# A two-layer hybrid decoder trunk on eight cores: 1/rms applied when PSUM is emptied, mixers reordered, one output projection, FFN results in a ring

## The reference

```
h    = rmsnorm(x) * g1                 # x * rsqrt(mean(x^2)+eps), over the 2048 channels
proj = h @ w_in                        # 2048 -> 4352 = 512 | 768 768 768 | 768 768
y_pool  = per group of 128: (window mean - token) @ pool_w * scale        # windows 2,4,8,16
y_sconv = B * causal_conv3(C * H)                                         # three 768 slices
y_cconv = silu(rmsnorm(causal_conv31(a * sigmoid(b)) + bias) * gc)        # norm over 768
x   += concat(y_pool, y_sconv, y_cconv) @ w_out
h2   = rmsnorm(x) * g2
up   = causal_conv3(h2 @ w_up)         # 2048 -> 2 x 5632
x   += (silu(up_left) * up_right) @ w_down
```

## Time and profile before

| | |
|---|---|
| time, median of 3 runs | 3723.16 us (3722.08 to 3724.32) |
| span of the profiled execution, slowest core | 3729.4 us |
| spans of the eight cores | 3711.1 to 3729.4 us |
| busy: PE, DVE, ACT, POOL | 3322.6, 2094.5, 531.7, 571.4 us |
| chain that ended last: PE, DVE, issue, DMA, ACT | 82%, 11%, 3%, 2%, 1% |
| w_up transfers: size, time to landing | 512 KB, 8.0 us |

### The profile page before, as it was taken

How to read it: one execution, slowest core, us unless ns; L and a number is a source line. 1 busy time by engine, 2 the same in 40 slices (tenths; PEclk the granted TensorE clock), 3 DMA queues, 4 the chain that set the end, 5 groups by cost and what they waited for, 6 DMA issues and landing times.

```text
span 3729.4 us, 51409 instructions; the slowest of 8 cores (3711.1 to 3729.4 us)
## 1 busy us (share of the span) xinstructions
PE 3322.6 (89%) x18974; PEld 1736.0 (47%) x19348; DVE 2094.5 (56%) x3179; ACT 531.7 (14%) x694; POOL 571.4 (15%) x602
## 2 busy tenths in 40 slices
PE   4799985799999999999859999768999999999994
PEld 3355442345555555445425554334555555544542
DVE  4533466566565565566564345657656555556556
ACT  2100002122011121112010000121212012011102
POOL 0111100111111211221201110010121121121120
PEclk7799998899999999999979999988999999999997
DMA  6276621467767767757717663144776766776752
GB/s 139 28 75 66 65 31 14 46 57 66 68 64 71 67 61 69 65 56 68 82 20 72 60 69 42 14 45 43 71 67 63 71 62 64 71 67 57 70 63 105
DMA packets 823905, 228.97 MB, mean 61 GB/s; under 512 B 809428, under 2 KB 821068, under 8 KB 821196
## 3 DMA queue, kind: packets, MB, share of 16 engines
q0 software_dynamic: 756064, 191.14, 55.7%
q1 hardware_dynamic: 63312, 32.75, 3.6%
q10 hardware_dynamic: 4284, 1.77, 0.2%
HBM read 402.17 MB, written 17.15 MB: 112 GB/s over the span
## 4 chain that ended last, share of the span: by engine, by line
PE 82%; DVE 11%; issue 3%; DMA 2%; ACT 1%; DVEq 0%; ACTq 0%; SPq 0%
PE pA L332 38%; PE pB L332 37%; DVE sb_hT L386 2%; PE pB L629 2%; PE pA L629 2%; DVE sb_sq L365 2%; DVE sb_rstd L380 1%; DVE sb_arena L496 1%; DVE sb_arena L642 1%; DVE sb_xT L787 1%; DMA sb_arena<-xp 1%; PE pA L374 1%; DVE sb_xT L807 1%; PE pB L374 0%; DMA o_ffn_s<-sb_arena 0%
## 5 line engine op out<-in xcount | busy, mean ns | idle before, releaser
L332 PE MATMUL pA<-sb_hT,sb_wr 128*128 128x512 bf16 (+1 forms) x5740 | 1017.0, 334 | 66.0 <-DVE sb_hT L386 35.1
L332 PE MATMUL pB<-sb_hT,sb_wr 128*128 128x512 bf16 (+1 forms) x5739 | 1014.0, 333 | 60.1 <-DVE sb_hT L386 32.3
L332 PEld LDWEIGHTS pA<-sb_hT,sb_wr 128*128 128x128 bf16 x5856 | 520.7, 99 | 542.7 <-issue 96.2
L332 PEld LDWEIGHTS pB<-sb_hT,sb_wr 128*128 128x128 bf16 x5856 | 519.3, 99 | 535.5 <-issue 87.5
L496 DVE SCALAR_TENSOR_TENSOR sb_arena<-sb_arena,sb_vecs 128x1056 f32<-128x1056 f32 x752 | 627.9, 835 | 80.3 <-DVE sb_arena L496 1.4
L332 PE MATMUL pB<-sb_arena,sb_wr 128*128 128x512 bf16 (+1 forms) x2819 | 521.7, 336 | 48.8 <-DVE sb_xT L787 28.3
L332 PE MATMUL pA<-sb_arena,sb_wr 128*128 128x512 bf16 (+1 forms) x2829 | 522.7, 337 | 46.8 <-DVE sb_xT L787 27.9
L332 PEld LDWEIGHTS pB<-sb_arena,sb_wr 128*128 128x128 bf16 x2880 | 259.2, 100 | 285.0 <-issue 68.0
L332 PEld LDWEIGHTS pA<-sb_arena,sb_wr 128*128 128x128 bf16 x2880 | 259.1, 100 | 285.0 <-issue 68.8
L320 POOL DMA_DIRECT2D sb_wr<-w_up x176 | 201.3, 1144 | 1155.2 <-PE pA L332 566.8
L320 POOL DMA_DIRECT2D sb_wr<-w_down x256 | 214.2, 839 | 738.5 <-PE pB L332 369.9
(11 more groups left out here) (96 smaller groups left out, 1468.8 us busy)
## 6 DMA issues: line engine op xcount, KB each, us to landing
sb_wr<-w_up POOLq DMA_DIRECT2D x176, 512.0 KB, 8.0
sb_wr<-w_in POOLq DMA_DIRECT2D x68, 512.0 KB, 7.2
sb_wr<-w_down POOLq DMA_DIRECT2D x128, 192.0 KB, 4.1
sb_wr<-w_down POOLq DMA_DIRECT2D x128, 160.0 KB, 3.8
sb_wr<-w_out POOLq DMA_DIRECT2D x64, 192.0 KB, 4.3
sb_arena<-xp SPq DMA_DIRECT2D x8, 1024.0 KB, 9.8
yp<-sb_arena SPq DMA_DIRECT2D x8, 1024.0 KB, 6.1
sb_wr<-w_out POOLq DMA_DIRECT2D x32, 128.0 KB, 3.5
```

What stands on the lines that cost most here:

```text
L332: S.op("pe", lambda e, k=k, c0=c0, n=n: e.matmul(ps[:, c0:c0 + n], lhsT=lhs_fn(k), rhs=rhs_fn(k)[:, c0:c0 + n], start=(k == 0), stop=(k == ...
```

## The change

**1/rms at eviction.** `hT` is written as x * g alone, on ACT (`h_part`), behind each addition to `xT`. The 1/rms, `R0`, is multiplied in on DVE when a PSUM tile is emptied (`mul_r`), or into the second factor of a product. ACT's copies out of PSUM go (FFN, pooling, C, and the sigmoid is taken from SBUF), and the first tap of the FFN convolution goes from DVE to ACT.

**Squares.** `SumSq.add` squares a block on ACT and adds it to a running sum on DVE, behind each chunk of the output projection and of the last down group; `finish` adds over channels with three matmuls, then square root and reciprocal. `mid_stats` puts `finish` behind the eighth block of the first chunk of the next stage. For the first layer the squares, the ones matmuls and the square root are taken per input tile, of which four instead of three are in flight.

**Order.** Conformer convolution first, then short convolution 0 to 2 with the conformer's norm in it, pooling 3 to 0, short convolution 3 to 5, then one output projection 16 blocks deep. The work buffers E are 1218 columns wide instead of 1704, and mixer and FFN results share a ring of 16 slots.

**FFN.** Down groups of 11, 11, 11, 5 and 6 pieces, each behind the up chunks that it needs, with no up group between. State loads and stores go by four pieces, the stores right behind the fourth.

The core of the diff (lines in their order, cut):

```
-GF = 6
+FG = [(0, 11), (11, 11), (22, 11), (33, 5), (38, 6)]
+NF = 44
...
+        deferred.clear()
+        for j, k in enumerate(order):
             for (c0, n) in BLKS:
...
+                S.op("pe", lambda e, j=j, k=k, c0=c0, n=n: e.matmul(
+                    ps[:, c0:c0 + n], lhsT=wr[:, base + k, :], rhs=rhs_fn(k)[:, c0:c0 + n],
+                    start=(j == 0), stop=(j == nk - 1)),
+                    reads=wres + rhs_res(k), writes=[psn])
+            if mid is not None and j == mid[0]:
+                mid[1]()
+        for f in pend:
+            f()
+        return psn
...
+    class SumSq:
+        def __init__(self, n, acc, sqs, fin, fin_res):
+            self.n, self.acc, self.sqs = n, acc, sqs
+            self.fin, self.fin_res = fin, fin_res
+            self.i = 0
+        def add(self, src, src_res):
+            i = self.i
+            self.i += 1
+            if i == 0:
+                act(self.acc.ap[:, 0:T], src, AF.Square, src_res, self.acc.res)
+                return
+            q = self.sqs[i % len(self.sqs)]
+            act(q.ap[:, 0:T], src, AF.Square, src_res, q.res)
+            last = i == self.n - 1
+            dve_tt(self.fin if last else self.acc.ap[:, 0:T], self.acc.ap[:, 0:T], q.ap[:, 0:T], ALU.add,
+                   self.acc.res + q.res, self.fin_res if last else self.acc.res)
+        def finish(self, out, out_res, inv_n):
+            psn = next_ps()
+            ps = PS[psn]
+            for (c0, n) in BLKS:
+                S.op("pe", lambda e, c0=c0, n=n: e.matmul(ps[:, c0:c0 + n], lhsT=onesB[:], rhs=self.fin[:, c0:c0 + n],
+                                                          start=True, stop=True),
+                     reads=self.fin_res + ["onesB"], writes=[psn])
+            act(out, ps[:, 0:T], AF.Sqrt, [psn, "epsT"], out_res, bias=epsT[:], scale=inv_n)
+            S.op("dve", lambda e: e.reciprocal(out=out, in_=out), reads=out_res, writes=out_res)
...
+    def norm_sum():
+        return SumSq(16, tb[1], [E[0], E[1]], E[2].ap.bitcast(BF16)[:, 0:T], E[2].res)
+    def h_part(gname, c):
+        act(hT[:, c, :], xT[:, c, :], AF.Copy, [("x", c), "vecs"], [("h", c)], scale=V(gname, c))
+    def add_x(psn, dc):
+        ps = PS[psn]
+        dve_tt(xT[:, dc, :], ps[:, 0:T], xT[:, dc, :], ALU.add, [psn, ("x", dc)], [("x", dc)])
...
+            xv = xT[:, half * 8:(half + 1) * 8, col0:col0 + n]
+            xres = [("x", c) for c in ks]
+            gv = V(("n1g", 0), half * 8, 8).unsqueeze(2).to_broadcast([128, 8, n])
+            dve_tt(hT[:, half * 8:(half + 1) * 8, col0:col0 + n], xv, gv, ALU.mult, xres + ["vecs"], [("h", c) for c in ks])
+            act(SQB[:, half * 8:(half + 1) * 8, 0:n], xv, AF.Square, xres, [("sqb", half)])
...
+            for kc in ks:
+                S.op("pe", lambda e, ck=ck, kc=kc, n=n: e.matmul(
+                    pC[:, ck * 512:ck * 512 + n], lhsT=onesB[:], rhs=SQB[:, kc, 0:n], start=(kc == 0), stop=(kc == 15)),
...
+        act(R0[:, col0:col0 + n], pC[:, ck * 512:ck * 512 + n], AF.Sqrt, [cres, "epsT"], ["R0"], bias=epsT[:], scale=1.0 / D)
+    S.op("dve", lambda e: e.reciprocal(out=R0[:], in_=R0[:]), reads=["R0"], writes=["R0"])
+    for b in E:
+        zero(b.ap, b.res + [("sqb", 0), ("sqb", 1)])
...
+        for (d0, dn, e0, sh) in ((0, NP, 0, 1), (NP, NS, s_off, 16)):
+            for i in range(3):
...
+                d = dst[:, d0:d0 + dn]
+                if i == 0 and first == "act":
+                    act(d, src, AF.Copy, ext_res + ["vecs"], dst_res, scale=w)
+                elif i == 0:
+                    dve_ts(d, src, w, ext_res + ["vecs"], dst_res)
...
+                    dve_stt(d, src, w, d, ext_res + ["vecs"] + dst_res, dst_res)
+    def mul_r(out, ps_ap, lo, hi, psn, res):
+        dve_tt(out, ps_ap, R0[:, lo:hi], ALU.mult, [psn, "R0"], res)
...
+            psn = proj(w_in_d, l, o4 + D_CC + i * 128, mid=mid_stats() if i == 0 else None)
...
+            act(Eb.ap[:, VS:VS + 480], pc, AF.Copy, cres, Eb.res)
+            mul_r(sg.ap, ps[:, 0:T], 0, T, psn, sg.res)
+            act(sg.ap, sg.ap, AF.Sigmoid, sg.res, sg.res)
+            for f in pending:
                 f()
...
+            dve_tt(sg.ap, sg.ap, R0[:], ALU.mult, sg.res + ["R0"], sg.res)
...
+        def sconv(i, after_c=(), after_h=(), l=l):
...
+            psn = proj(w_in_d, l, o1 + D_SC + i * 128)
...
+            mul_r(g.ap, ps[:, 0:T], 0, T, psn, g.res)
+            dve_tt(g.ap, g.ap, R0[:], ALU.mult, g.res + ["R0"], g.res)
+            for f in after_c:
...
+            psn = proj(w_in_d, l, o1 + 2 * D_SC + i * 128)
...
+            dve_tt(g.ap, g.ap, R0[:], ALU.mult, g.res + ["R0"], g.res)
+            for f in after_h:
+                f()
+            psn = proj(w_in_d, l, o1 + i * 128)
...
+        sconv(0, after_c=pending[:])
+        pending.clear()
+        deferred.append(lambda: csum.finish(tb[1].ap, tb[1].res, 1.0 / D_CC))
+        sconv(1, after_c=[lambda: cc_norm_out(0)], after_h=[lambda: cc_norm_out(1)])
+        sconv(2, after_c=[lambda: cc_norm_out(2), lambda: cc_norm_out(3)], after_h=[lambda: cc_norm_out(4), lambda: cc_norm_out(5)])
+        for b in PE_:
+            zero(b.ap[:, 0:16], b.res)
+        for g in (3, 2, 1, 0):
+            pool_group(g)
...
+        for i in range(3, 6):
+            sconv(i)
...
+        order = [10 + i for i in range(6)] + [0, 1, 2, 3] + [4 + i for i in range(6)]
...
+        for dc in range(16):
+            psn = chunk(wcols(w_out_d, l, 0, 16, dc * 128), 16, order,
+                        lambda k: slot(kslot[k]), lambda k: slres(kslot[k]))
+            add_x(psn, dc)
+            nsum.add(xT[:, dc, :], [("x", dc)])
+            h_part(("n2g", l), dc)
...
+                if ectr["i"] <= 3:
+                    zero(Eb.ap[:, 0:2], Eb.res)
+                psn = proj(w_up_d, l, side * D_FF + f * 128, mid=mid_stats() if first else None)
+                ps = PS[psn]
+                mul_r(Eb.ap[:, 2:2 + NP], ps[:, 0:NP], 0, NP, psn, Eb.res)
+                mul_r(Eb.ap[:, FS_OFF + 32:FS_OFF + 160], ps[:, NP:T], NP, T, psn, Eb.res)
+                S.op("dve", lambda e, Eb=Eb, ch=ch: e.transpose(out=oT3[:, ch, :], in_=Eb.ap[:, FS_OFF + 128:FS_OFF + 160]),
+                     reads=Eb.res, writes=oTX.res)
...
+                conv3(tb[side].ap, Eb.ap, FS_OFF, "fw", l, uc, Eb.res, tb[side].res, "act")
+                if side == 0:
+                    act(tb[0].ap, tb[0].ap, AF.Silu, tb[0].res, tb[0].res)
+            m = f % 16
+            dve_tt(slot(m), tb[0].ap, tb[1].ap, ALU.mult, tb[0].res + tb[1].res, slres(m))
+            if fi == 3:
...
+        def ffn_down(g, nxt, l=l):
+            f0, nf = FG[g]
+            last = g == len(FG) - 1
+            ns = norm_sum() if last else None
...
+                psn = chunk(w_down_d[l, f0 * 128:(f0 + nf) * 128, dc * 128:(dc + 1) * 128].rearrange("(kc p) c -> p kc c", p=128),
+                            nf, range(nf), lambda k: slot((f0 + k) % 16), lambda k: slres((f0 + k) % 16))
+                add_x(psn, dc)
+                if last:
+                    ns.add(xT[:, dc, :], [("x", dc)])
+                    if nxt is not None:
+                        h_part(nxt, dc)
+            if last:
+                pre_stats.append(ns)
...
+        nxt = ("n1g", l + 1) if l + 1 < DEPTH else None
+        done = 0
+        for (lo, hi, downs) in ((0, 12, [0]), (12, 23, [1]), (23, 34, [2]), (34, 44, [3, 4])):
+            for f in range(lo, hi):
+                ffn_up(f)
+            for g in downs:
+                ffn_down(g, nxt)
...
+    flush_deferred()
+    pre_stats.pop().finish(R0[:], ["R0"], 1.0 / D)
...
```

657 lines of the change are left out of this document (253 added, 404 removed).

## The result

| | before | after |
|---|---|---|
| median of the runs | 3723.74 us | 3583.48 us |
| undisturbed runs | 3722.08, 3723.16, 3724.32 | 3568.73, 3577.34, 3589.61 |
| ratio, 95% interval | | 0.960 (0.955 to 0.965) |
| profiled execution: span | 3729.4 us | 3575.8 us |

The change makes the kernel 4.0% faster: 145 us by the means of the undisturbed runs (3723.2 and 3578.6), 154 by the two profiled executions; forecast were 218.

The account below looks back on a forecast made before the run. PE was taken as the bound, busy 3322.6 of 3729.4 us, losing time to idling and a slow clock. Gains of 308 less costs of 90 made 218: 3511, less 6, 3505 us; range 3445 to 3590.

Parts of the forecast that it names:

- conformer stage: Conformer convolution: sigmoid wait goes, DVE turn about 34.5 us against PE's 30; gain 10 us (-10 to 25), both layers.
- pooling: Pooling stage: sums covered by later chunks, eviction behind the previous group's sums on DVE; 15 us lost, gain 30.
- squares: Last down group: DVE's addition, wait for square and sum take 4.27 us, chunks 5.0 with slow clock; cost 64 us.
- norms (three): Second norm (twice) and first norm of layer 1: first chunk starts at once, 10.9 us lost each; gain 109.
- start: First layer's input load ends at 72 us, second chunk starts at 87 instead of 112.5; gain 25 us (17 to 37).
- conformer norm: Norm behind the conformer: 12 us wait for the next chunk but one, 1.7 slow, 0.8 more; gain 51 us.
- FFN groups, eviction, stores: FFN: group-start losses shrink, gain 67; DVE eviction hidden at 7.85 against 8.01 us, 0; four-piece stores cost 26 (0 to 100).
- end: Final norm and output: 31.7 us becomes 15.7; gain 16 us.
- The forecast's 80: FFN loss before the change: 56.2 us of waits at down groups' third chunks plus 14 slow starts of 1.7 us.
- rival B: FFN: DVE becomes the bound, mildly, at 8.9 us per up chunk; 158 us more, 3663 us; chance 0.12.
- Rival C: Last down group runs at 1.2 GHz throughout; 32 us more, 3537 us; chance 0.13.
- E: Rival: FFN stores land in time and the last down group's clock holds; 26 and 24 less, 3455 us; chance 0.12.

Follow-up runs that it names:

- The two runs on this stage: Kernel after with ACT's emptying of the prompt taps behind the first decode tap, 3532.9 us; the same with decode taps between the matrices, 3496.6 us.
- E0: Not a run: the pooling stage's buffer, into which ACT copies the state and DVE writes the eviction's product.
- reordered conformer stage: Kernel after with each conformer decode tap directly behind its diagonal matrix and ACT's emptying of the prompt taps behind them: 3496.6 us.

## Why the prediction came out 78 us too low

The direction held, and the time lies inside the range, 7 us from its slow end; of 218 us 145 came. The conformer stage lost where a gain was forecast, pooling and the FFN gave less than forecast, and that the time still lies inside the range is partly luck: the squares were priced 36 us too dear, and had they cost the 64 of the forecast, the time would have been near 3619, beyond the range. Of the forecast's own signs of being wrong two came, up chunks more than 8.01 us apart away from the stores and longer waits in the conformer stage; the load (71.3 us) and the waits for o_ffn_s (8, 14.2 us in all) stayed within theirs. The profiled executions, both read in the same way, give this for two layers:

| term | forecast | measured | how |
|---|---|---|---|
| norms (three) | +109 | +102 | lost 12.3, 12.3 and 14.5 instead of 10.9 each |
| start | +25 | +30 | second chunk at 82.3, not 87 |
| conformer norm | +51 | +38 | lost 21 instead of 14.5 |
| conformer stage | +10 | -32 | lost 47 per layer where it was 31; turns of 39.2, not 34.5 |
| pooling | +30 | +7 | lost 27.5 where it was 31; stage of 61.5, not 48.5 |
| FFN groups, eviction, stores | +67, 0, -26 | +17 | loss of 72 where it was 88.5 |
| squares, last down group | -64 | -28 | 4.13 us for twelve chunks per layer, 3.0 for four; not 5.0 for all |
| end | +16 | +15 | 19.6 us to the first scaled block, the output 3 shorter |
| sum | +218 | +149 | the spans differ by 154; 5 are in no term |

The FFN's loss is the time from the third up chunk to the end of the last down group (689.2 to 1782.1 and 2412.9 to 3503.1), less 86 chunks of 8.01 and 704 blocks of 0.50 us, less the squares: 37.2 and 34.7, 72 in all. The squares' part is what the last group's sixteen chunks take beyond 3.0 us each: 1720.1 to 1782.1 less 48.1, 14 us per layer. Before, the FFN's stretch was 755.7 to 1851.3 and 2547.9 to 3640.2 us less 87 chunks and the same blocks: 45.9 and 42.6, so 88.5. The forecast's 80 had only the waits for `xT`'s additions and their slow chunks. The conformer's is 82.3 to 318.8 us less 13 chunks and six times 14.3 us of taps, 46.5 (48.0 in layer 1, with 12 chunks); with the same 14.3, the 213.0 us of the earlier trace rows lost 31, not the 34 that the forecast had with 13.9.

**Norms and conformer norm: right. Start: nearly the time, by another way.** The waits of 8.28 and 11.65 us answer to the 8.1 and 12 that the steps gave. Only the slow chunk behind them was dearer, 2.7 to 2.8 us instead of the 1.7 of the earlier trace rows, where PE had waited 3.56 us. The conformer norm also has a wait of 3.88 us ahead of its first transposes (330.82) and a slow chunk, where the steps had 0.8. At the start PE waited for no eviction, where the forecast had the second chunk behind reciprocal and eviction: the sums stand in pC there, so pB was free at once, and pA was emptied before the third chunk's turn at 90.28; what was lost was the slow first chunk of 10.73 us.

**Conformer stage: the step that failed.** "About 34.5 us against PE's 30" was 39.2 (five turns, 114.85 to 310.75). It added DVE's instructions, but left out a wait that the change makes: the first decode tap now stands behind ACT's emptying of the prompt taps (2.83 us, 34.1 in all), since both write one slot. It also took PE's share as fixed, though PE, once it waits, runs its transposes and taps slowly: 15.3 to 16.4 us for taps that take 14.5. The two runs on this stage show both: 3 us less of wait before the transposes of each turn gave 47 us, and a chain within PE's pace gave 84 and a clock of 1.00. What the stage lost before did go (no wait for the sigmoid is left); the change put 47 us in its place.

**Pooling: a wait not seen.** The step had DVE's sums as the only thing ahead of the eviction. The eviction's product into E0 is ordered behind ACT's copy of the state into E0, and that copy stands in ACT's queue behind `pool_mm`'s emptying, which waits for DVE's sums of the group before. So each group waited for all of the one before it. With the order turned, the stage takes 47.1 us, and the forecast was 48.5.

**FFN groups and eviction: 0.16 us to spare were not there.** The sum used 1.05 and 0.25 us for ACT's two first taps; 1.05 is the length of a plain copy. With a scale from memory they take 1.18 and 0.40 us, and DVE waits 1.0 and 0.6 us for them, 258.8 in all. A piece then takes 16.37 us of DVE (PE's rows at 770.34 and 786.71) where PE needs 16.03. PE pays for this late: in layer 0 its up chunks follow each other every 8.01 us in most places, all 44 ahead of the second and third down groups among them, and are late by 8.2 us in all at the others. DVE falls 0.17 us behind per chunk, the two PSUM tiles hide it, and the next down group's start collects it: the three groups of 11, forecast free, lose 6.4, 4.2 and 5.2 us in waits and slow chunks, and the group of 5 loses 13.2 instead of 6.6. The tap on DVE, where it was before the change, gave 25 us back. So rival B had its mechanism, at 8.18 us per chunk of DVE and not at 8.9: by the tap's run, a sixth of its 158 us. The Trainium skill ("ScalarE: Activation LUTs", "What ACT_TABLE_LOAD costs") states 93 ns more for each operand that is a pointer per partition; the trace agrees roughly, with 0.13 us more than the plain copy of 1056 columns, though that copy read PSUM and the tap reads SBUF, so the operand's share is not isolated.

**Stores: mis-sized.** 26 forecast, 18 measured by leaving them out.

**Squares: mis-sized, in the kernel's favour.** The first four chunks of the group still came every 3.0 us; the twelve others lasted the 4.13 us that DVE's queue makes (4.27 by the sum), and the clock held. The stretch in the last down group, kernel after (start:end, length, busy PE, PEld, DVE, ACT, POOL, clock, DMA share, GB/s):

```profile
1732.00:1782.00 50.00, 38.20 (x218) 18.56 (x216) 32.32 (x24) 28.36 (x24) 7.83 (x9) 1.00 0.62 60
```

PE paused 0.97 us in every 4.13 and was granted 2.4 GHz throughout. The Trainium skill ("TensorE: Matmul & The Clock Gate", on the second HAM failure mode) warns of just such pauses between groups; by its strongest reading, an estimate, the term was 96. The trace doesn't agree here, and the measurement decides: 28. Rival C falls, and the half of E that says the clock holds was right.

## What to carry to other kernels

When work moves from one engine to another, list for each instruction what it is ordered behind by *name*, not by data: in the conformer and pooling stages DVE waited for a small piece of ACT's work in another part of the same buffer, and moving one line gave 47 and 34 us. A margin of 2% on the second engine (7.85 against 8.01 us) is none: estimate it with the form that the change issues, scale and bias included. And take an instruction that waits for another engine out of the queue ahead of an eviction: the reciprocal cost its 7.5 us and the wait for the root. And where an engine builds operands at another's pace, its idle time between them is the place for its other work.

## What the runs showed of the hardware

- ACT with a scale per partition, out of SBUF, took 1.18 us for 1056 columns and 0.40 for 128; a plain copy of 1056 out of PSUM took 1.05.
- A wait of PE of 2.15 us before a chunk left the chunk at 8.17 us; 2.93 us were followed by a loss of 1.4, 8.28 and 11.65 us by 2.7 and 2.8. The length of the wait alone does not decide it: behind two waits of 2.65 us one chunk took its 5.67 us and one 7.35. Pauses of 0.97 us in 4.13, twelve in a row, cost no clock at all.
- In the reordered conformer stage PE was busy for 210.0 of 220 us at a clock of 1.00, and DVE with 129.5 us of work in it held nothing up.
